# Moving the keys' input and its shift columns out of a shared tensor in a fused two-block kernel

## The reference, cut to what matters

```python
def _shared_kv(x, cs, kv_norm_g, kv_mod_w, kv_mod_b, w_kv):
    shift, scale = jnp.split(cs @ kv_mod_w + kv_mod_b, 2, axis=-1)
    h = _modulate(_rmsnorm(x, kv_norm_g), shift, scale)   # h*(1+scale)+shift
    k, v = jnp.split(h @ w_kv, 2, axis=-1)
```

```python
def swiglu_ffn(h, w_gate, w_up, w_down):
    return (jax.nn.silu(h @ w_gate) * (h @ w_up)) @ w_down
```

## Time and profile before

| | |
|---|---|
| median of 3 runs | 753.21 us (753.13 to 753.42) |
| the profiled execution | 753.22 us |
| its span | 751.3 us |
| PE matmul busy | 724.5 us, 96%, 3,898 matmuls |
| PE weight loads busy | 626.4 us, 83%, 3,898 |
| DVE busy | 509.6 us, 68% |
| ACT busy | 396.2 us, 53% |
| moved by DMA | 156.65 MB |

### The profile page before, as it was taken

One profiled execution on the slowest core, in us unless ns is written; L12 is line 12 of the kernel. 1 busy time (PEld: TensorE's weight loads), 2 busy tenths in 40 slices (PEclk: granted clock), 3 DMA queues, 4 the chain that ended last, 5 costly groups with the idle time before them and its releaser, 6 DMA issues.

```text
span 751.3 us, 9715 instructions
## 1 busy us (share of the span) xinstructions
PE 724.5 (96%) x3898; PEld 626.4 (83%) x3898; DVE 509.6 (68%) x794; ACT 396.2 (53%) x622; POOL 2.4 (0%) x8
## 2 busy tenths in 40 slices
PE   2999999999899999999999999999999999999996
PEld 2888889999899999878888888888788888888885
DVE  5889997998876989986744545454576544545444
ACT  4157446864875677755644344433665344344423
POOL 0000000000000000000000000000000000000000
PEclk9999999999999999999999999999999999999999
DMA  8999983899643525213755445544226455455201
GB/s 339 425 427 413 425 361 147 305 388 348 273 134 149 205 91 210 84 36 161 280 174 203 182 171 198 191 167 172 109 112 224 168 183 205 172 173 198 77 0 57
DMA packets 23229, 156.65 MB, mean 208 GB/s; under 512 B 2576, under 2 KB 2832, under 8 KB 5264
## 3 DMA queue, kind: packets, MB, share of 16 engines
q1 hardware_dynamic: 22608, 153.41, 54.1%
q0 software_dynamic: 576, 2.62, 1.0%
HBM read 154.97 MB, written 1.05 MB: 208 GB/s over the span
## 4 chain that ended last, share of the span: by engine, by line
PE 80%; DVE 10%; ACT 6%; issue 2%; DMA 2%; SPq 0%; DVEq 0%; ACTq 0%
PE pb L1562 20%; PE pb L1563 19%; PE pb L1564 19%; PE pb L1636 13%; DVE w L1009 4%; PE pb L1832 2%; ACT w L611 2%; PE pb L1933 1%; DVE raw L1012 1%; DMA raw<-w_dram 1%; DMA x<-x_dram 1%; DVE t L1009 1%; DVE x L1012 1%; PE pb L1863 1%; PE pb L1875 0%
## 5 line engine op out<-in xcount | busy, mean ns | idle before, releaser
L1009 DVE TENSOR_TENSOR w<-raw,w 128x2048 fp32r<-128x2048 f32 x97 | 221.2, 2290 | 143.6 <-ACT w L611 143.6
L611 ACT ACTIVATE w<-raw 128x2048 fp32r<-128x2048 f32 x97 | 184.8, 1912 | 143.3 <-PE pb L1564 119.2
L1562 PE MATMUL pb<-w,r 128*128 128x512 f32 (+1 forms) x640 | 246.5, 385 | 0.7 <-DVE r L1012 0.4
L1563 PE MATMUL pb<-w,r 128*128 128x512 f32 (+1 forms) x640 | 243.3, 380 | 0.0
L1564 PE MATMUL pb<-w,r 128*128 128x512 f32 (+1 forms) x640 | 243.2, 380 | 0.0
L1562 PEld LDWEIGHTS pb<-w,r 128*128 128x128 f32 x640 | 120.5, 188 | 25.6 <-issue 1.8
L1564 PEld LDWEIGHTS pb<-w,r 128*128 128x128 f32 x640 | 120.5, 188 | 24.7
L1563 PEld LDWEIGHTS pb<-w,r 128*128 128x128 f32 x640 | 120.6, 188 | 23.3
L1562 PE MATMUL pb<-r,w 128*128 128x256 f32 (+1 forms) x352 | 100.3, 285 | 1.0 <-DVE r L1009 0.5
L1563 PE MATMUL pb<-r,w 128*128 128x256 f32 (+1 forms) x352 | 99.4, 282 | 0.0
L1564 PE MATMUL pb<-r,w 128*128 128x256 f32 (+1 forms) x352 | 99.0, 281 | 0.0
(11 more groups left out here) (191 smaller groups left out, 582.6 us busy)
## 6 DMA issues: line engine op xcount, KB each, us to landing
raw<-w_dram SPq DMA_DIRECT2D x129, 1024.0 KB, 4.9
ow<-w_dram SPq DMA_DIRECT2D x8, 1024.0 KB, 15.2
ow<-w_dram SPq DMA_DIRECT2D x8, 512.0 KB, 16.7
oh<-w_dram SPq DMA_DIRECT2D x2, 1024.0 KB, 22.6
x<-x_dram SPq DMA_DIRECT2D x2, 512.0 KB, 5.7
f<-rc_dram POOLq DMA_DIRECT2D x1, 1024.0 KB, 5.0
acc<-row_dram POOLq DMA_DIRECT2D x2, 512.0 KB, 5.2
out_dram<-f SPq DMA_DIRECT2D x4, 256.0 KB, 2.3
```

The source lines that it names most:

```text
L611: return e.activation(out, in_, ACT.Copy, **kw)
L1009: return e.tensor_tensor(out, a, b, op)
L1562: e.matmul(out, a_hi, b_hi, start=start, stop=False)
L1563: e.matmul(out, a_hi, b_lo, start=False, stop=False)
```

## The change

The high part of the keys' input and its shift columns get a place of their own, `KR`, 8 rows of 272 words, of which 258 are used: 256 tokens, the shift's high part and the shift's low part. KR lies where `F0` lies; the placeholder `upto` (12,288 words) makes it so. R2 has rows of 256 words again and holds, for the keys, only the low parts. `gap` is gone, and as R2 is 32 words smaller, all tensors behind it stand 128 bytes lower: in the built program ow and w0 start at byte 16,512 of a partition before and after, oh and r2 at 82,048, the first raw buffer at 114,944 before and 114,816 after, x at 155,904 and 155,776.

```diff
-            OW, OH, _, H0, S1 = [... ("ow", (NSPL, 2, 2048)), ("oh", (2, 2048)), ("gap", (32,)),
-                ("h0", (12, T)), ("s1", (D,)))]
+            OW, OH, H0, S1 = [... ("ow", (NSPL, 2, 2048)), ("oh", (2, 2048)), ("h0", (12, T)),
+                ("s1", (D,)), ("upto", (12288,)))][0:4]
+            KR = early.enter_context(nc.sbuf_tensor("kr", [P, 8, 272], f32r))
-        R2 = sb("r2", [P, RT, 2, T + 2], f32r)
+        R2 = sb("r2", [P, RT, 2, T], f32r)
+        k2 = sb("k2", [P, 2])
...
+        def raw_key(d):
+            return KR[:, d, 0:T + 2]
+        raw_shift = KR[:, :, T:T + 2]
...
-            for c in range(2):
-                done = copy(R2[:, :, 0, T + c], mv[:, 4, :])
-            done.then_inc(s_shh, 1)
+            copy(raw_shift[:, :, 0], mv[:, 4, :]).then_inc(s_shh, 1)
...
-                e.activation(hi_of(R2, d), X[:, d, :], ACT.Copy, scale=mv[:, 3, d:d + 1]).then_inc(s_khi, 1)
+                e.activation(raw_key(d)[:, 0:T], X[:, d, :], ACT.Copy, scale=mv[:, 3, d:d + 1]).then_inc(s_khi, 1)
...
-                    copy(kb[:, d:d + 1], bank_of("k", d)[:, T:T + 1]).then_inc(s_kb, 1)
+                    copy(k2[:, :], bank_of("k", d)[:, T:T + 2], accum_out=kb[:, d:d + 1]).then_inc(s_kb, 1)
...
-            for c in range(2):
-                done = tt_(R2[:, :, 1, T + c], mv[:, 4, :], R2[:, :, 0, T + c].bitcast(f32), SUB)
-            done.then_inc(s_shl, 1)
+            tt_(raw_shift[:, :, 1], mv[:, 4, :], raw_shift[:, :, 0].bitcast(f32), SUB).then_inc(s_shl, 1)
...
-                    done = product(bank_of(*name)[:, 0:T + 2], w[:, 0, o:o + P], w[:, 1, o:o + P], R2[:, kt, 0, :],
-                                   R2[:, kt, 1, :], kt == 0, kt == KT - 1)
+                    with_shift = bank_of(*name)[:, 0:T + 2]
+                    e.matmul(with_shift, w[:, 0, o:o + P], raw_key(kt), start=kt == 0, stop=False)
+                    e.matmul(with_shift, w[:, 1, o:o + P], raw_key(kt), start=False, stop=False)
+                    done = e.matmul(out_of(*name), w[:, 0, o:o + P], lo_of(R2, kt), start=False, stop=kt == KT - 1)
```

More of the change, by code:

```diff
@@ L340, in two_block_program @@
         with ExitStack() as early:
-            OW, OH, _, H0, S1 = [early.enter_context(nc.sbuf_tensor(name, [P, *shape], f32)) for name, shape in (
-                ("ow", (NSPL, 2, 2048)), ("oh", (2, 2048)), ("gap", (32,)), ("h0", (12, T)), ("s1", (D,)))]
+            OW, OH, H0, S1 = [early.enter_context(nc.sbuf_tensor(name, [P, *shape], f32)) for name, shape in (
+                ("ow", (NSPL, 2, 2048)), ("oh", (2, 2048)), ("h0", (12, T)), ("s1", (D,)), ("upto", (12288,)))][0:4]
+            KR = early.enter_context(nc.sbuf_tensor("kr", [P, 8, 272], f32r))
         W = [sb(f"w{i}", [P, 2, 2048], f32r) for i in range(NSPL)]
-        R2 = sb("r2", [P, RT, 2, T + 2], f32r)
+        R2 = sb("r2", [P, RT, 2, T], f32r)
         R1 = sb("r1", [P, 8, 2, T], f32r)
@@ L478, in half_of @@
             return R[:, kt, h, a * P:a * P + P]
+        def raw_key(d):
+            return KR[:, d, 0:T + 2]
+        raw_shift = KR[:, :, T:T + 2]
         def hi_of(R, i):
-            return R[:, i, 0, 0:T]
+            return R[:, i, 0, :]
         def lo_of(R, i):
-            return R[:, i, 1, 0:T]
+            return R[:, i, 1, :]
         def ended(*name):
@@ L958, in hidden_high @@
                     p.wait_ge(*slab_ended(AT["d", layer, i - 4]))
-                copy(R2[:, r:r + 2, 0, 0:T], bank_of("ht", layer, i)[:, :].rearrange("p (j n) -> p j n",
+                copy(R2[:, r:r + 2, 0, :], bank_of("ht", layer, i)[:, :].rearrange("p (j n) -> p j n",
                                                                                    j=2)).then_inc(s_ghi, 1)
@@ L1222, in _ @@
             p.wait_ge(s_shh, 1)
-            for c in range(2):
-                done = tt_(R2[:, :, 1, T + c], mv[:, 4, :], R2[:, :, 0, T + c].bitcast(f32), SUB)
-            done.then_inc(s_shl, 1)
+            tt_(raw_shift[:, :, 1], mv[:, 4, :], raw_shift[:, :, 0].bitcast(f32), SUB).then_inc(s_shl, 1)
             def key_low(d):
                 p.wait_ge(s_khi, d + 1)
-                stt(lo_of(R2, d), X[:, d, :], mv[:, 3, d:d + 1], hi_of(R2, d).bitcast(f32), MUL, SUB).then_inc(s_klo, 1)
+                stt(lo_of(R2, d), X[:, d, :], mv[:, 3, d:d + 1], raw_key(d)[:, 0:T].bitcast(f32), MUL,
+                    SUB).then_inc(s_klo, 1)
             for d in range(8):
@@ L1481, in hidden_low @@
                 p.wait_ge(s_ghi, n + 1)
-                tt_(R2[:, r:r + 2, 1, 0:T], bank_of("ht", layer, i)[:, :].rearrange("p (j n) -> p j n", j=2),
-                    R2[:, r:r + 2, 0, 0:T].bitcast(f32), SUB).then_inc(s_glo, 1)
+                tt_(R2[:, r:r + 2, 1, :], bank_of("ht", layer, i)[:, :].rearrange("p (j n) -> p j n", j=2),
+                    R2[:, r:r + 2, 0, :].bitcast(f32), SUB).then_inc(s_glo, 1)
             def ffn(layer, *name):
@@ L1575, in tile_of @@
                 cs = slice(o + half * P, o + half * P + P)
-                return product(out, w[:, 0, cs], w[:, 1, cs], hi_of(R, r), lo_of(R, r), start, stop)
+                return product(out, w[:, 0, cs], w[:, 1, cs], R[:, r, 0, :], R[:, r, 1, :], start, stop)
             def single(k, names, R, ready, base, r0=0, n_k=8, first=True, last=True, tok=False):
```

## The result

The changed kernel takes 746.10 us (median of 4 runs, 746.01 to 746.59); the kernel before, on the same chip, 753.32 us (4 runs, 753.13 to 753.83). The ratio is 0.9904 with a 95% interval of 0.9887 to 0.9922. I had forecast 753.14 us with a range of 752.7 to 754.0: the kernel is 7.2 us faster where I expected nothing. The profiled execution took 746.59 us, its span 744.8 us against 751.3.

The account below looks back on a forecast made before the run. TensorE (PE), busy 96% of the span, was taken to bound the kernel. 753.22 us less 0.05 for columns and 0.03 for pitch, nothing for shift columns, bias and places, gave 753.14 us; range 752.7 to 754.0.

Parts of the forecast that it names:

- Everything behind R2 lies 128 bytes lower: Tensors behind R2: no dependence of engine instructions on their new places, DMA no slower off 256 bytes; taken at 0.
- the one on the down projection: Sign of being wrong: the down projection's step, expected at 231 ns, moves by more than 1 ns.
- The pitch term: All readers of R2: its pitch of 1,024 bytes instead of 1,032 gains 0.03 us, with ends 0 and 0.07.
- my pair for it: Down projection with R2 as weights, 230.9 ns, against gate and up with R1, 232.3: no pitch cost to win back.
- My rival on the pitch: About 1,200 matmuls reading R2: pitch costs more than pairs show, 1.3 ns each, giving 751.6 us; chance 0.02.
- The other pair: Queries with R2 moving, 118.7 ns, against values with R1, 118.6: odd pitch costs at most 0.1 ns a matmul.
- a price of the odd pitch: 224 low-part matmuls: 65 lines touched for 64, 1.9 ns each, 0.4 us in all; not used in the sum.
- columns: Key products: two columns fewer in one matmul of three, 0.8 ns on each of 64, saving 0.05 us.
- shift columns: One 128x8 copy on ACT and one subtraction on DVE go, about 0.15 and 0.13 us; nothing for PE.
- bias: Accumulated key bias on ACT: 0.7 to 1.5 us, taken at 1.5, hidden by ACT's waits for PE; nothing late.
- PE's wait at the queries: PE's wait before the first query matmul: stays near 0.5 us; over 0.7 us would show the forecast wrong.
- The DMA rival: Transfers through raw buffers slow down at the new address, 0 to 5.2% on 32.6 exposed us, up to 754.9; chance 0.05.

Follow-up runs that it names:

- e4: The changed kernel with 32 unused words behind R1, putting raw and the rest on a multiple of 256 bytes as before; 745.91 us.
- e1: The changed kernel with 32 unused words ahead of R1, so R1 and everything behind it stand as before; 751.63 us, ratio 0.9975.
- e2: The kernel before, R2's pitch still 1,032 bytes, with 32 more unused words behind R2, moving R1 and raw to 128 past 256; 748.46 us, ratio 0.9937.
- e8: The changed kernel with 32 unused words ahead of W and 32 ahead of R1: W, R2 on a multiple of 256 bytes, R1 128 past; 751.51 us.
- e10: The kernel before with the change's keys (KR, narrower low part, accumulated bias), every place and R2's pitch as before; 753.71 us, ratio 1.0000.
- e9: The changed kernel with two views of R1 and R2: distance 0 from W for 512-column products, 64 bytes off for 256-column ones; 744.76 us, ratio 0.9878.
- e6: The changed kernel with 16 unused words ahead of R2 and 16 behind R1, R1 and R2 64 bytes off W; 754.72 us, ratio 1.0018.

## Why the prediction was wrong

**The step that failed** is "Everything behind R2 lies 128 bytes lower": "No engine instruction shows a dependence on that", taken at 0. It is worth -6.53 us in the wide products by R1's place (e4 against e1) and +0.57 by raw's; e2, with these places alone, is 4.7 us faster than before by the ratio (5.3 by the medians of its chip), and 6.00 us in the wide part. I looked for the dependence only in each tensor's own start, and asked it only of DMA. The numbers for the right question stood in my own text: W at byte 16,512, and R1, by the sizes 16,512 bytes behind R2's 82,048, an odd multiple of 128 away from W before and a multiple of 256 after. What counts is that distance, and e8 shows it against the absolute place. Of my signs of being wrong the one on the down projection fired (more than 1 ns; 230.9 to 228.7 in the same stretch); the step of gate and up, where most of the gain is, was not among them.

**The pitch term**, taken at -0.03 us, measured -2.02 us in the wide part (e1). The mechanism I had named, R2's odd rows costing its readers, was there, but my pair for it was spoiled. I compared down with R2 (230.9 ns) against gate and up with R1 (232.3) and took R1 for the undisturbed member. R1 had a penalty of its own, 5.7 ns, and so the pair showed two penalties and their difference. The undisturbed step is 226.7 ns, and my stretch of 23 steps of down had 11 of the longer ones of its first half in it. My rival on the pitch, with a chance of 0.02, said that only an effect common to both members could hide its cost. What hid it was not common but a second one of like size on the other member. The rival's price, 751.6 us, and e1's 751.63, which has the pitch without the places, agree by luck: it wanted 1.3 ns on each of 1,200 matmuls, and the runs show some 4 ns on each of the 528 of the down projections and nothing won on the narrow ones. The other pair, 118.7 against 118.6 ns, was not like for like either: in the queries R2 moves, in the values R1 holds the weights and 256 columns of W move (the rows say `pb<-r,w` and `pb<-w,r`). The pitch costs nothing on the narrow products all the same: they became slower with the even pitch (118.7 to 119.8 ns in the queries).

Pitch and place may be one thing. With a pitch of 1,032 bytes each row of R2 stands 8 bytes further from W modulo 256 than the row ahead of it, so all rows but the first are at distances off 0. This is an argument; no run tests it.

By the 16-byte lines of the Trainium skill, SBUF — State Buffer, "Door 1: The DMA port swizzle", I had estimated a price of the odd pitch. The runs do not follow that estimate: on the narrow products the odd pitch saved 1.1 ns, and on the wide ones R1 rows that begin on whole lines cost as much (232.4 ns at 128 bytes, 233.3 at 64) as R2's odd ones (231.9).

**Right:** the keys' part, in that it does nothing that can be measured. e10's 1.0000 is the sum of columns, shift columns and bias; the 0.05 us of the columns did not show (keys 24.10 us for 24.09). The bias was over-priced, 0.7 us for my 1.5, and hidden by the wait at the second value's copy (0.68 us), not at the third as I wrote. PE's wait at the queries was 0.4 us for 0.5.

**The DMA rival** was right that transfers slow down in the changed kernel, at the low end of its bounds (1% of 0 to 5.2%), but it takes ow and raw both at 128 (e8 against after). It was wrong about the exposure: e4 without it is 0.2 us faster by the medians, inside its scatter. The rule of the Trainium skill, DMA: Bandwidth & Descriptors, "How a descriptor splits into AXI transactions", asks for one transaction in 32 more, an estimate of 3%. The packets of 20 to 95 us show a third of it at the most, and their median nothing of it where only ow (before) or only raw (e8) is off a multiple of 256.

**Open.** Why weights and moving rows disturb each other by their distance modulo 256, and why 512 columns want distance 0 where 256 columns are faster at 32 or 64; what else sets the step of 256 columns (the values of e10 and of e9); why raw's place costs 0.57 us in the down projections. Distances other than 0, 32, 64 and 128 were not tried.

## What to carry to other kernels

When a kernel is bound by matmuls, read the start-to-start step of each kind of product and compare it with the best step of that shape in any kernel, not with a neighbour that may be disturbed too. A change of one tensor's size moves all behind it: write down where each pair that is read together, weights and moving rows, stands modulo 256 before and after, and try a gap of some words as an experiment of its own before crediting the edit. Here 128 bytes of padding in the kernel before gave 4.7 of the 7.2 us, by the ratio.

## What the runs showed of the hardware

- A matmul of 128x128 weights by 512 columns in the 32-bit format of this kernel takes 226.7 ns from start to start when weights and moving rows are a multiple of 256 bytes apart, 232.4 at 128 and 233.3 to 233.4 at 32 and 64. At 0 the steps are even (standard deviation 0.5 ns), at 128 they scatter (3.8 ns).
- The same product with weights in rows of 1,032 bytes takes 231.7 ns in the second half of a down projection, for 226.7 with rows of 1,024 (11 steps in 16 slabs).
- For 256 columns the queries' stretch of 192 matmuls took 23.13 us at 0, 22.83 at 32, and 22.52 (e6) and 22.94 (e9, with longer waits) at 64. The values took 117.8 ns a step in e6 and 114.3 in e9 at the same distance.
- 8 KB DMA packets between 20 and 95 us take 312 to 313 ns in the median when their targets ow and raw both stand 128 bytes past a multiple of 256, and 309 when either or both stand on one.
- An accumulator read behind a small copy on ACT adds 0.09 us to the copy's own spacing, though it is listed with 0.19 us.
